# Second in-projection: twelve of 36 column units through Strassen's seven products, the rest in a new order

## The reference, cut to what matters

```python
h = rmsnorm(h_res, norm_w) * (1 + scale) + shift
proj = h @ w_in + b_in                # (2048 x 1024) @ (1024 x 4624)
(na_q, na_k, na_v, na_z, ml_q, ml_k, ml_v, ml_o, ml_z, i_f, f_f, i_b, f_b) = split(proj)   # nine of 512, four of 4
na_out = neighbourhood_attention(na_q, na_k, na_v, rpb) * silu(na_z)
mq, mk = split(silu(centred_short_conv([ml_q, ml_k])))          # five taps over tokens
hm = mlstm(mq, mk, ml_v, i_f, f_f) + flipped mlstm(..., i_b, f_b)  # chunk states over 64 tokens
hm = hm * sigmoid(ml_o)
ml_out = layernorm(hm) * ml_norm_w * silu(ml_z)
y = [na_out, ml_out] @ w_out
```

## Time and profile before

| | |
|---|---|
| time, median of 3 runs | 1885.39 us (1884.79 to 1885.74) |
| span of the profiled execution | 1883.3 us |
| its own device time | not recorded; the median is 2.1 us above the span |
| PE busy | 1865.6 us, 99% of the span |
| DVE, ACT, POOL busy | 982.4, 618.3, 552.5 us |
| moved by DMA | 303.55 MB, mean 161 GB/s |
| granted TensorE clock, mean of the span | 0.999 of full |

### The profile page before, as it was taken

The page is one execution under the profiler, slowest core; times in us unless marked ns, Lnnn a source line. Parts: engine busy times, 40 slices in busy tenths (PEclk is TensorE's granted clock), DMA queues, the critical chain, the costliest instruction groups (busy, mean ns, idle before and its releaser), DMA issues.

```text
span 1883.3 us, 26698 instructions
## 1 busy us (share of the span) xinstructions
PE 1865.6 (99%) x10035; PEld 1540.4 (82%) x10035; DVE 982.4 (52%) x2117; ACT 618.3 (33%) x1317; POOL 552.5 (29%) x925
## 2 busy tenths in 40 slices
PE   9999999999999999999999999999999999999998
PEld 8888878888888888888888787888887777788886
DVE  6556565775666433114777322223213777776665
ACT  7321111233444432101222202221114667655552
POOL 2112222233642222110110000222314777544442
PEclk9999999999999999999999999999999999999999
DMA  6223142366897745312221123665563776867663
GB/s 197 95 79 119 62 128 81 104 184 235 306 266 252 235 168 162 101 50 84 74 78 68 53 62 116 211 211 171 168 220 105 243 232 224 271 219 241 230 229 112
DMA packets 236365, 303.55 MB, mean 161 GB/s; under 512 B 41414, under 2 KB 161126, under 8 KB 236204
## 3 DMA queue, kind: packets, MB, share of 16 engines
q1 hardware_dynamic: 205724, 215.84, 37.4%
q0 software_dynamic: 23600, 77.61, 11.4%
q10 hardware_dynamic: 6912, 8.39, 1.2%
HBM read 194.71 MB, written 107.54 MB: 160 GB/s over the span
## 4 chain that ended last, share of the span: by engine, by line
PE 94%; DVE 2%; DMA 2%; issue 1%; ACT 1%; POOL 0%; SPq 0%; POOLq 0%; DVEq 0%; ACTq 0%
PE banks L145 25%; PE banks L147 25%; PE banks L146 25%; PE banks L2106 3%; PE banks L2069 3%; PE banks L2088 3%; PE banks L2704 2%; PE banks L2706 1%; PE banks L2397 1%; DMA iraw<-in_w_in 1%; PE banks L2089 1%; PE banks L2674 1%; PE banks L234 1%; PE banks L1109 1%; PE banks L1741 0%
## 5 line engine op out<-in xcount | busy, mean ns | idle before, releaser
L145 PE MATMUL banks<-hT,wu 128*128 128x512 f32 (+1 forms) x528 | 204.6, 387 | 1.1 <-DVE wu L512 0.6
L147 PE MATMUL banks<-hT,wu 128*128 128x512 f32 (+1 forms) x528 | 202.3, 383 | 0.0
L146 PE MATMUL banks<-hT,wu 128*128 128x512 f32 (+1 forms) x528 | 202.2, 383 | 0.0
L145 PE MATMUL banks<-iT,wub 128*128 128x512 f32 x384 | 151.2, 394 | 0.0
L145 PE MATMUL banks<-iT,wua 128*128 128x512 f32 x384 | 150.8, 393 | 0.0
L145 PE MATMUL banks<-wub,iT 128*128 128x512 f32 x384 | 150.6, 392 | 0.0
L147 PE MATMUL banks<-iT,wub 128*128 128x512 f32 x384 | 149.7, 390 | 0.0
L147 PE MATMUL banks<-iT,wua 128*128 128x512 f32 x384 | 149.5, 389 | 0.0
L146 PE MATMUL banks<-wub,iT 128*128 128x512 f32 x384 | 149.5, 389 | 0.0
L147 PE MATMUL banks<-wub,iT 128*128 128x512 f32 x384 | 149.5, 389 | 0.0
L146 PE MATMUL banks<-iT,wua 128*128 128x512 f32 x384 | 149.5, 389 | 0.0
(11 more groups left out here) (293 smaller groups left out, 4116.3 us busy)
## 6 DMA issues: line engine op xcount, KB each, us to landing
iraw<-in_w_in SPq DMA_DIRECT2D x36, 512.0 KB, 4.4
wa<-in_w_ada SPq DMA_DIRECT2D x48, 256.0 KB
yT<-sg POOLq DMA_DIRECT2D x32, 256.0 KB, 3.1
oraw<-yT SPq DMA_DIRECT2D x32, 256.0 KB, 4.8
xr<-in_x SPq DMA_DIRECT2D x16, 512.0 KB, 4.4
h<-h POOLq DMA_DIRECT2D x16, 512.0 KB, 4.3
hT<-tr POOLq DMA_DIRECT2D x16, 512.0 KB, 5.1
tws<-wg SPq DMA_DIRECT2D x16, 512.0 KB, 5.1
```

Of the source, the lines that this page charges most:

```text
L145: e.matmul(ps, lh, rh, start=first, stop=False)
L146: e.matmul(ps, lh, rl, start=False, stop=False)
L147: return e.matmul(ps, ll, rh, start=False, stop=last)
```

## The change

It does three things. First, the twelve units of `nq`, `nk` and `mz` leave `Proj` and are made after `mo` by a new class `Fast` with Strassen's scheme: two by two units of columns, two token blocks and the two halves of the features form 2 x 2 matrices, and seven products (numbered 1 to 7) of 12 matmuls each take the place of eight. There are 6 doubles (pairs of units for both `q`) of 14 steps, 84 steps `j` in all, three doubles for each half of the tokens, with `mz` last in each. The result tiles are combined in DVE (`summed`, `low`) from the banks and a `part` tile. Second, the operands are sums of quarters of the weights and of the tokens. Nine weight sums (512 KB each) and eight token sums (1 MB each) are made in memory by the DMA engines during the gates, `mk` and `mq`, one for each step: SP copies one quarter (`copy`, steps 21 to 37), POOL adds the other with an accumulating DMA (`add`, steps 26 to 42). The other sums are made on DVE. The splits of a step's weights are issued four (DVE) and five (ACT) steps ahead, those of the first token quarters in `mo`. Third, the remaining 24 units come in a new order (`PLAN`), in five slots (`SLOT`): `nz` and one unit of `mk`, the gates, `mk` and half of `mq`, `mk`'s last unit, `mv` (steps 44 to 59), one unit of `mq` (60 to 63), `nv` (64 to 79), one unit of `mq` (80 to 83), `mo` (84 to 99). `Gates` begins at step 45 and `States` at step 63, so that it runs through `nv`, the last unit of `mq`, and `mo` to tile 10, instead of `nz`, `mz` and `mo`; SP issues the state's transfers ahead of the stores of `nv` and of the weight loads. The loads of the attention move from `mo` into `Fast` (steps 72, 74, 78, 80), its `invert(0)` behind the last `summed`, and `Fast`'s own loads stand in `mo` (after tiles 2, 3, 7 and 11: 2, 2, 3 and 2 MB). Code now comes in one block more.

PE's matmuls go from 9112 to 8968 in the program: 144 groups of 24 become 96 groups and 84 products of 12.

```diff
+PLAN = [("nz", 0), ("nz", 1), ("nz", 2), ("nz", 3), ("mk", 0), ("mk", 1), ("mk", 2), ("mq", 0), ("mq", 1), ("mk", 3),
+        ("mv", 0), ("mv", 1), ("mv", 2), ("mv", 3), ("mq", 2), ("nv", 0), ("nv", 1), ("nv", 2), ("nv", 3), ("mq", 3),
+        ("mo", 0), ("mo", 1), ("mo", 2), ("mo", 3)]
...
 class Proj:
...
 
-    NU = 6
+    FIRST = 5
+    SLOT = (0, 1, 2, 3, 4, 0, 1, 2, 3, 0, 1, 2, 3, 4, 0, 1, 2, 3, 4, 0, 1, 2, 3, 4)
...
+            while nu < len(PLAN) and self.freed[self.prior[nu]] <= n + 1:
...
+        self.g0 = g0 = next(n for n, x in enumerate(work) if x[0] == "mv")
...
                     e.dma_start(self.br[:, x, :], io["b_in_2"][0, b * W:(b + 1) * W].partition_broadcast(P)).then_inc(*self.row_in.inc())
                 e.dma_start(self.wgr[:], self.win[:, :, 36 * P:36 * P + 16]).then_inc(*self.wg_in.inc())
+            fast.copy(e, w, n)
+            states.sp(e, w, n)
             if name == "nv":
...
-            states.sp(e, w, n)
...
+class Fast:
...
+    N, ND, OUTS, SLOTS = 84, 6, 48, 10
+
+    SEQ = [(i, q) for i, q in ((5, 0), (5, 1), (2, 0), (2, 1), (1, 0), (3, 0), (1, 1), (3, 1), (4, 0), (4, 1), (6, 0), (6, 1), (7, 0), (7, 1))]
+    LEFT = {1: ((0, 0), (1, 1)), 2: ((1, 0), (1, 1)), 3: ((0, 0), None), 4: ((1, 1), None),
+            5: ((0, 0), (0, 1)), 6: ((1, 0), (0, 0)), 7: ((0, 1), (1, 1))}
+    RIGHT = {1: ((0, 0), (1, 1)), 2: ((0, 0), None), 3: ((0, 1), (1, 1)), 4: ((1, 0), (0, 0)),
+             5: ((1, 1), None), 6: ((0, 0), (0, 1)), 7: ((1, 0), (1, 1))}
+    DOUBLES = [(("nq", 0), ("nk", 0)), (("nq", 2), ("nk", 2)), (("mz", 0), ("mz", 2))]
+    ORDER = [(0, 0), (0, 1), (0, 2), (1, 0), (1, 1), (1, 2)]
+    BLOCKS, LONG, ADDED = ("nq", "nk", "mz"), (5, 2, 6, 7), (1, 6, 7)
...
+        self.early_x = {6: (0, 5), 7: (0, 2), 11: (0, 1), 12: (0, 3), 14: (0, 4), 15: (0, 6)}
+        self.late_x = {4: (0, 7), 33: (1, 5), 35: (1, 2), 38: (1, 1), 40: (1, 3), 42: (1, 4), 45: (1, 6), 48: (1, 7)}
...
+    SUMS = 17
+
+    def copy(self, e, w, n):
+
+        n -= 21
+        if 0 <= n < self.SUMS:
+            w.wait_ge(*self.proj.full.ge(n + 21))
+            if n >= 3:
+                w.wait_ge(*self.copy_in[n % 3].ge(n // 3))
+            dst, src, _ = self.sums(n)
+            e.dma_start(dst, src).then_inc(*self.copy_in[n % 3].inc())
+
+    def add(self, e, w, n):
+
+        n -= 26
+        if 0 <= n < self.SUMS:
+            w.wait_ge(*self.copy_in[n % 3].ge(n // 3 + 1))
+            dst, _, src = self.sums(n)
+            e.dma_start(dst, src, accum_op=ALU.add).then_inc(*self.added.inc())
...
+    def tokens_load(self, e, w, half, i):
+
+        a, b = self.LEFT[i]
+        s = self.x_in[i - 1]
+        if half:
+            w.wait_ge(*self.full.ge(self.x_done[i]))
+        if i in self.LONG:
+            w.wait_ge(*self.added.ge(self.SUMS))
+            e.dma_start(self.xa[i][:], self.hs[half, self.LONG.index(i)].rearrange("(k p) t -> p k t", p=P)).then_inc(*s.inc())
+            return
+        self.quarter_load(e, self.xa[i], half, a, s)
+        if b is not None:
+            self.quarter_load(e, self.xb[i], half, b, s)
...
+    def early_sp(self, e, w, m):
+        proj = self.proj
+        if m == 2:
+            w.wait_ge(*proj.lo.ge(len(proj.jobs)))
+            self.unit_load(e, self.rx, 0, 0, self.rx_in)
+            for i in range(2):
+                w.wait_ge(*proj.ca_st[i].ge(16))
+            self.unit_load(e, self.r0, 0, 1, self.rx_in)
+        for i in {3: (5, 2), 7: (1, 3), 11: (4, 6)}.get(m, ()):
+            w.wait_ge(*proj.full.ge(proj.mo0 + m + 1))
+            self.tokens_load(e, w, 0, i)
+
...
+            for j in range(4):
+                self.weights_high(e, w, j)
+
+    def early_dve(self, e, w, m):
+        if m == 10:
+            self.tokens_difference(e, w, 0)
+        if m in self.early_x:
+            self.tokens_low(e, w, *self.early_x[m])
+        if m == 14:
+            for j in range(4):
+                self.weights_low(e, w, j)
...
+    def act(self, e, att):
+        w = Waits(e)
+        self.weights_high(e, w, 4)
+        for j in range(self.N):
+            i, q = self.SEQ[j % 14]
+            if j + 5 < self.N:
+                self.weights_high(e, w, j + 5)
+            if j == self.N - 1:
+                att.first_act(e, w)
+            if i == 5:
+                w.wait_ge(*self.full.ge(j + 1))
+                w.wait_ge(*self.proj.row_step.ge(48))
+                w.wait_ge(*self.o_z.ge(self.z_at[8 * (j // 14) - 1]))
+                e.activation(self.part[q][:], self.pp[q], ACT.Copy).then_inc(*self.copied.inc())
+            elif j in self.at:
+                self.high(e, w, self.at[j])
+            if j in self.late_x:
+                self.tokens_high(e, w, *self.late_x[j])
...
+    def summed(self, e, w, o):
+
+        name, _, _, q = self.block(o)
+        lo, ps, part = self.so[o % 3][1], self.bank(o), self.part[q]
+        w.wait_ge(*self.full.ge(14 * (o // 8) + self.OUT_AT[o % 8][0] + 1))
+        w.wait_ge(*self.w_out.ge(4 * (o // 8) + 4))
+        self.buffer_free(w, o)
+        op = ALU.subtract if o % 8 < 6 else ALU.add
+        if name == "nq":
+            for y in range(2):
+                e.scalar_tensor_tensor(out=self.into(lo[:], y), in0=self.turned(ps, y), scalar=-1.0, in1=self.turned(part[:], y),
+                                       op0=ALU.mult, op1=op).then_inc(*self.o_z.inc())
+        else:
+            e.scalar_tensor_tensor(out=lo[:], in0=ps, scalar=-1.0, in1=part[:], op0=ALU.mult, op1=op).then_inc(*self.o_z.inc())
...
+    def dve(self, e, att):
+        w = Waits(e)
+        self.weights_sum(e, w, 5)
+        for j in range(self.N):
+            n, p = divmod(j, 14)
+            i, q = self.SEQ[p]
+            before = self.at.get(j - 1)
+            if before is not None and before % 8 >= 4:
+                self.low(e, w, before)
+            if j == self.N - 1:
+                att.first_dve(e, w)
+            part = self.part[q]
+            if i == 5:
+                pass
+            elif i == 2:
+                w.wait_ge(*self.full.ge(j + 1))
+                w.wait_ge(*self.copied.ge(2 * n + q + 1))
+                e.tensor_tensor(part[:], self.pq[q], part[:], ALU.subtract).then_inc(*self.w_out.inc())
+            elif i == 1:
+                w.wait_ge(*self.full.ge(j + 1))
+                w.wait_ge(*self.w_out.ge(4 * n + q + 1))
+                e.tensor_tensor(part[:], self.pr, part[:], ALU.add).then_inc(*self.w_out.inc())
+            elif self.at[j] % 8 < 4:
+                self.low(e, w, self.at[j])
+            else:
+                self.summed(e, w, self.at[j])
+            if j == self.N - 1:
+                att.invert(e, w, 0)
+            if j + 4 < self.N:
+                self.weights_low(e, w, j + 4)
+            if j + 6 < self.N:
+                self.weights_sum(e, w, j + 6)
+            if j - 1 in self.late_x:
+                self.tokens_low(e, w, *self.late_x[j - 1])
+            if j == 37:
+                self.tokens_difference(e, w, 1)
+        self.low(e, w, self.OUTS - 1)
+
...
+        if m in (72, 74):
+            fast.stored(w, 32)
+            w.wait_ge(*fast.full.ge(m))
             for j in self.jobs:
-                if j[0] == "q":
+                if j[0] == "q" and j[2] < 2 and j[1] // 2 == (m - 72) // 2:
                     self.load(e, w, 0, j)
-        if m == 7:
-            proj.stored_all(w, "nz")
-            proj.stored_all(w, "nv")
-            w.wait_ge(*full)
-            for j in self.jobs:
-                if j[0] in ("z", "v"):
-                    self.load(e, w, 0, j)
-            self.values(e, w, 0)
-            self.values(e, w, 1)
-        if m == 11:
-            w.wait_ge(*full)
+        if m == 74:
+            fast.weighed(w)
             for j in self.jobs:
                 if j[0] == "t":
                     self.load(e, w, 0, j)
+            fast.stored(w, 40)
+            for j in self.jobs:
...
-        self.invert(e, w, 0)
...
+        if m == 80:
+            w.wait_ge(*self.fast.full.ge(m))
             for part in range(4):
                 self.block(e, w, 0, part)
...
-        self.g0 = proj.nv0 + 3
-        self.s0 = proj.nv0 + 21
+        self.g0 = proj.g0 + 1
+        self.s0 = self.g0 + 18
```

More of the change, by code:

```diff
@@ L1287, in __init__ @@
         self.rawn = {n: i for i, n in enumerate(n for n, j in enumerate(jobs) if j[0] != "gates" and n not in self.passing)}
-        self.freed = {}
-        for n, (name, u, tb) in enumerate(work):
-            if name == "gates":
-                continue
-            for x in range(4 if name in ROW_BLOCKS else 1):
-                self.freed[u + x] = n + 1
-        self.stage, nst, self.convs = {}, 0, {}
+        self.stage, self.convs = {}, {}
         for n, (name, u, tb) in enumerate(work):
@@ L1447, in early_sp @@
             self.load(e, w, n)
+        if m == 15:
+            self.load(e, w, self.job[("w", 1)])
         if m == 12:
@@ L2295, in sp @@
         if n == self.g0 - 1:
```

(8 more changed lines are left out.)

591 lines of the change are left out of this document (435 added, 156 removed).

## The result

The changed kernel takes 1915.76 us (1914.46 to 1920.12, 4 runs) against 1885.57 (1884.79 to 1887.79, 4 runs): ratio 1.0161, 95% interval 1.0147 to 1.0176, 30.2 us slower. The prediction was 1884.5 with a range of 1873 to 1900, so it was wrong. The profiled execution of the changed kernel took 1915.7, its span is 1913.9.

The account below looks back on a forecast made before the run. PE was taken as the bound, busy 1865.6 of 1883.3 us. The products' -32.6 us and the added waits and clock terms summed to -0.8, so 1885.4 became 1884.5 us, range 1873 to 1900.

Parts of the forecast that it names:

- DMAs that add in memory: Sums made in memory by accumulating DMAs: +1 us taken, by the loads' rate; upper bound 17 left at 9 us per MB.
- the clock: Matmuls behind long PE gaps run at 1.2 GHz; three gaps counted as long enough, +3 us.
- The products: PE's matmuls: 144 fewer at 0.2267 us each, -32.6 us, called sure.
- The end of `mv`: PE waits 4.0 us for `mpB` against 1.8 at the gates' start; with a later first state product, +3.4 us.
- The end of `nv`: Convolution behind four splits and ahead of the state's update makes PE wait 12.6 us; with the next steps +13.3.
- Loads in `mo`: `Fast`'s loads delay the state's `CD` behind tiles 7 and 3: 8.5 us by measured burst, 0.7 by queue rate, +5 taken.
- Start of `Fast`: `tokens_low` of the fourth operand and four weight splits stand behind `mo`'s last Sigmoid, about +1 us.
- into the attention: From `Fast` to the attention, ACT's Silus, Copies and table loads start the third exponential pair 5.8 us behind, not 2.7: +3.1.
- DVE in `Fast`: DVE has 47 us of work in 43.6 us of products in the second token half: +1 us (0 to 6).
- stores of `nv`: Stores of `nv` beside the state's transfers: +1 us (0 to 4).
- rival C: Adding DMAs are slow, at 9 us per MB they hold POOL's convolution stores: +17, 1901 us; chance 0.14.
- my sign for being wrong: Among the signs of a wrong forecast: an adding DMA's time from issue to landing passes 5.4 us per MB.

Follow-up runs that it names:

- e3_late: Changed kernel with two of the four weight loads behind `mv` and `nv` one step later, and the splits one and two steps later; 1904.51 us.
- e6_spaced_loads: Changed kernel with `Fast`'s token loads in `mo` issued one MB at a time instead of two or three; 1907.0 us.
- e1_plain: Changed kernel with its 17 adding DMAs made plain copies of the same source to the same place; 1894.55 us.
- e4_act_stores: Changed kernel with the convolution's stores issued by ACT behind its Silu, in ACT's queue instead of POOL's; 1931.1 us.
- e11: Changed kernel with four result tiles `ca` instead of two for convolutions 4 to 23; 1910.4 us.
- e13: Changed kernel with sums every second step from 7, four `ca` tiles for convolutions 4 to 19, later splits, `mo` loads one MB each; 1884.35 us.
- e14_mixed: Changed kernel with four `ca` tiles (convolutions 4 to 19), early sums, token sums three steps apart, later splits, `mo` loads one MB each; 1882.58 us.

## Why the prediction was wrong

The forecast sum was -0.8; measured are +30.2. The step that failed is the term for the DMAs that add in memory, taken as +1, where 17.4 us of waits and 3.9 of lower clock stand; the second is the clock, +3 for 14.0. By its steps:

- *The products*, -32.6: right. 144 matmuls less in the trace.
- *The end of `mv`*, +3.4: the wait right, 4.1 us for `mpB` (4.0 forecast); with the steps behind it PE idles 6.9 us from 940 to 1000, 5.1 more than the 1.8 of the earlier trace rows, so this term is 1.7 more than taken. That is the first state product, 2.4 us for 1.2.
- *The end of `nv`*, 12.6 of waiting: right, 12.5. The last split ends 17.8 us behind the bias sum (17.7 forecast), and e3_late, which moves the splits and half of the loads behind the first convolution, takes away 7.7 of the 13.3 us measured there. The rest stayed in every order that I tried (5.0 to 6.3 us).
- *Loads in `mo`*: 6.7 measured, 5 taken, 8.5 by the measured burst, 0.7 by the rate of the whole queue. The burst was the better row, though behind tile 7 it gave 6.7 for 3.8 and behind tile 3 1.8 for 2.9; e6_spaced_loads shows the mechanism. One reading was wrong: `CD<-state` is the store of the state, not a load. The next update waits until it has landed, so the wait is as forecast. And the formula that I set against the burst is one for DMAs that GpSimd issues, while these are SP's.
- *Start of `Fast`* 0.8 for 1; *into the attention* 3.7 us against 0.8 before, +2.9 for 3.1.
- *DVE in `Fast`* 0.6 for 1; *stores of `nv`*: no wait that I can put down to them, for 1.
- *DMAs that add in memory*, +1: the step that failed. It was mis-sized by 16.4 us of waits and 3.9 of clock. I chose the lower end "by the loads' rate", a row of another kind of transfer; rival C, which had the way (late stores, two `ca` tiles), got a chance of 0.14. That its upper bound gave 17 is luck. It has eight adds of 9 us; POOL issues the eight adds of 1 MB 7.0 us apart (816.64 to 865.69), and 8 x (7.0 - 5.44) = 12.5 would leave 1.6 over the free 10.9. What it left out is the nine weight sums, beside which the convolutions had already lost 18.6 of the 31.1 us. (A small slip there: from 7.2 us per MB on, 14.1 - 10.9 is 3.2, not 3.8.) And my sign for being wrong, landing after more than 5.4 us per MB, does not separate the cases: the plain copies of e1_plain land after 8.5 and cost 2.1 us. e1_plain shows that the adding is the price, e4_act_stores that another queue for the stores does not help, e11 and e13 that the loss reaches PE by two ways, late stores and late raw weights, through a convolution chain with 0.14 us of slack in 21.76. e14_mixed, with both mended and the large sums three steps apart, has none of the 17.4 left. That slack could be read before the run and was not.
- *The clock*, +3: mis-sized. 14.0 us. I counted three gaps; there were two more at the convolutions' end (3.9), and the way into the attention, where no gap is longer than 2.2 us, cost most, 4.4: PE waits there for 2.20 and 1.35 us, and the windows from 1470 on are at 0.61, 0.50 and 0.86. The row at the run's end showed the fall, but not that a gap of 2.2 us can go before one.

The two errors (16.4 and 11.0) and the 2.9 us of busy time that I can't place are 30.3 of the 31.3 us by which the forecast missed; the other terms' errors (+3.4 and -1.8) are small beside them.

## What to carry to other kernels

A DMA that adds in memory is not a load with another operator: price it by a row of its own kind, count the small ones too, and if no row has it, take the dearer end or measure one first. Ask of every chain that keeps pace with PE how much slack it has in one round; one that has 0.14 us of 21.76 passes on every delay of a store, however far PE seems from it. And where a change puts several waits on PE, count for each what the clock takes afterwards, here 14 us on 46.
